# Ten dense projections per layer by seven half-size products each, with the sums of their weights added up in HBM by accumulating DMAs from GpSimd

## The reference

```python
for l in range(DEPTH):                      # DEPTH = 2
    h = rms_norm_2(x, norm_w[l])            # (256, 1024)
    x = x + hybrid_mixer(h, w_in[l], ...)

def hybrid_mixer(h, w_in, ...):
    proj = h @ w_in                         # (256, 1024) @ (1024, 5648)
    qkv, z_a, a_lg, b_lg, cf_val, cf_glu, z_b, gate_lg = jnp.split(proj, pts, axis=-1)
    qkv = jax.nn.silu(depthwise_conv_centred(qkv, qkv_conv_w))        # 5 taps
    ...                                     # gated delta rule, forward and backward -> o
    y_a = (o * silu(z_a)) @ w_dn_out        # (256, 512) @ (512, 1024)
    u = cf_val * jax.nn.sigmoid(cf_glu)
    u = depthwise_conv_centred(u, cf_conv_w) + cf_conv_b              # 31 taps
    u = jax.nn.silu(layer_norm_2(u, cf_ln_w, cf_ln_b))
    y_b = (u * jax.nn.silu(z_b)) @ w_cf_out
    gate = jax.nn.sigmoid(gate_lg + gate_b).reshape(bsz, seq, N_BRANCH, D_MODEL)
    y = gate[:, :, 0] * y_a + gate[:, :, 1] * y_b
    return y @ w_out
```

## Time and profile before

| | |
|---|---|
| Runs shown | 1493.84 and 1493.32 us, median 1493.58 |
| Span of the profiled execution | 1491.9 us, from the first to the last instruction |
| PE busy | 1459.9 us, 98% of the span |
| DVE, ACT, POOL busy | 57%, 30%, 21% |
| DMA | 184.4 MB at 124 GB/s on the mean |

### The profile page before, as it was taken

How to read it: one execution, slowest core, us unless ns; L and a number is a source line. 1 busy time by engine, 2 the same in 40 slices (tenths; PEclk the granted TensorE clock), 3 DMA queues, 4 the chain that set the end, 5 groups by cost and what they waited for, 6 DMA issues and landing times.

```text
span 1491.9 us, 21689 instructions
## 1 busy us (share of the span) xinstructions
PE 1459.9 (98%) x8912; PEld 1187.2 (80%) x8912; DVE 852.3 (57%) x1685; ACT 450.8 (30%) x905; POOL 311.3 (21%) x310
## 2 busy tenths in 40 slices
PE   7999999999999999999999999899999999999998
PEld 2677777667788888755968998788888888888887
DVE  1376666664544357623757744546688344677835
ACT  1232355424112121222326430233333213333321
POOL 0223302210666442131110402110100131010012
PEclk9999999999999999999999999999999999999999
DMA  9632232201322213331333353433332334333231
GB/s 387 255 139 113 114 113 114 114 29 54 143 95 98 92 57 116 144 113 57 114 113 114 114 227 113 159 143 139 114 115 100 123 130 154 128 114 115 113 114 43
DMA packets 17958, 184.39 MB, mean 124 GB/s; under 512 B 2370, under 2 KB 2882, under 8 KB 5316
## 3 DMA queue, kind: packets, MB, share of 16 engines
q1 hardware_dynamic: 17860, 183.01, 32.2%
HBM read 181.95 MB, written 1.05 MB: 123 GB/s over the span
## 4 chain that ended last, share of the span: by engine, by line
PE 89%; ACT 3%; DVE 3%; issue 1%; POOL 1%; DMA 1%; SPq 0%; DVEq 0%; POOLq 0%; ACTq 0%
PE ps L910 86%; PE ps L965 4%; DVE arena L2041 1%; DVE arena L2035 1%; DMA arena<-in_rp 1%; POOL arena L2848 1%; ACT arena L1559 0%; POOL arena L2852 0%; ACT L1995 0%; ACT L1993 0%; DMA arena<-in_wf 0%; DVE arena L2257 0%; DVE arena L2456 0%; ACT arena L1589 0%; ACT arena L1993 0%
## 5 line engine op out<-in xcount | busy, mean ns | idle before, releaser
L910 PE MATMUL ps<-arena 128*128 128x256 f32 (+7 forms) x8420 | 1411.5, 350 | 16.3 <-DMA arena<-in_wf 6.6
L910 PEld LDWEIGHTS ps<-arena 128*128 128x128 f32 (+4 forms) x8420 | 1133.9, 179 | 263.0 <-issue 126.6
L2848 POOL TENSOR_TENSOR arena<-arena 128x256 f32<-128x256 f32 (+6 forms) x254 | 280.3, 1124 | 855.3 <-DVE arena L2041 303.8
L2035 DVE TENSOR_TENSOR arena<-arena 128x512 f32<-128x512 f32 (+9 forms) x346 | 300.3, 893 | 176.1 <-ACT arena L1559 96.9
L1559 ACT ACTIVATE arena<-ps 128x512 f32<-128x512 f32 (+2 forms) x355 | 166.2, 489 | 569.9 <-PE ps L910 513.9
L2041 DVE SCALAR_TENSOR_TENSOR arena<-arena 128x256 f32<-128x256 f32 (+4 forms) x496 | 238.7, 532 | 106.7 <-ACT arena L1589 24.2
L2035 DVE TENSOR_TENSOR arena<-ps,arena 128x512 f32<-128x512 f32 (+16 forms) x157 | 64.5, 432 | 91.4 <-PE ps L910 81.4
L2041 DVE SCALAR_TENSOR_TENSOR arena<-arena,ps 128x256 f32<-128x256 f32 (+2 forms) x103 | 43.8, 439 | 80.7 <-PE ps L910 60.1
L965 PEld LDWEIGHTS ps<-arena 128*128 128x128 f32 x488 | 56.1, 142 | 33.5 <-issue 15.3
L965 PE MATMUL ps<-arena 128*128 128x128 f32 x488 | 73.4, 280 | 8.3 <-ACT arena L1559 5.5
L2038 DVE TENSOR_SCALAR arena<-arena 128x256 f32<-128x256 f32 (+10 forms) x179 | 62.1, 380 | 13.7 <-POOL arena L2848 10.8
(11 more groups left out here) (96 smaller groups left out, 299.8 us busy)
## 6 DMA issues: line engine op xcount, KB each, us to landing
arena<-in_wf SPq DMA_DIRECT2D x68, 2048.0 KB, 7.6
arena<-in_wf SPq DMA_DIRECT2D x22, 1024.0 KB, 6.5
arena<-in_first SPq DMA_DIRECT2D x3, 1024.0 KB, 20.6
arena<-in_wf SPq DMA_DIRECT2D x2, 1152.0 KB, 11.9
arena<-in_xin SPq DMA_DIRECT2D x4, 512.0 KB, 5.2
arena<-in_rp SPq DMA_DIRECT2D x2, 1024.0 KB, 10.1
arena<-in_consts SPq DMA_DIRECT2D x1, 1410.0 KB, 23.1
arena<-in_pa SPq DMA_DIRECT2D x2, 532.0 KB
```

The lines of the kernel that those rows point to most:

```text
L910: return e.matmul(o, l, r, start=start, stop=stop, skip_group_check=True)
L2035: return e.tensor_tensor(o, x, y, op)
L2848: return e.tensor_tensor(o, x, y, op)
```

## The change

Ten pieces of each b layer (`q1`, `q2`, `cv`, `cg`, `za`, `zb`, `m00`, `m10`, `m01`, `m11`, in this new order; `ab` and `q0` stay) are computed by seven products each. A product is 8 matmuls of 128 by 128 weights with 128 tokens, so a piece is 56 such matmuls in place of 32 with 256 tokens. A dense step is now two products (the fourth one only), and the order string stays. Products 6 and 5, 3 go on adding to the PSUM bank of product 1, and product 4 to that of product 7, after ACT has copied the value so far; DVE adds what belongs together (three adds of 128 x 256 a piece), and makes four sums of tokens (128 x 512 each) at the start of each layer.

The four sums of weights that the scheme wants for each piece (S1 to S4, 0.5 MB each) are made in HBM: GpSimd issues for two pieces at a time one plain DMA (HBM to HBM, 4 MB, one quarter of the weights written to all four sums) and three accumulating ones (3 MB, 3 MB and 1 MB), each after a wait for the one before. These 40 DMAs stand at fixed places of GpSimd's order: 13 and 12 in the two a layers (`KEEP_A`), one behind each of the groups of adds in their merges (`KEEP_M`), and 7 in the first b layer (`KEEP_B`). SP loads quarters and sums one by one, 70 loads of 0.5 MB in a b layer in place of 10 of 2 MB; the loads of sums of a pair of pieces wait for that pair's four DMAs. The ring is cut finer (14 places of 1024 columns), and from the first b layer on 12 places are left, the other two hold the sums of tokens. Beside this the squares of the second branch's layer norm go to four buffers in place of one, and some semaphores are shared.

```diff
-UNIT = 2048
-NU = 7
+UNIT = 1024
+NU = 14
...
+SEVEN_B = [("q1", "A"), ("q2", "A"), ("cv", "A"), ("cg", "C"), ("za", "T"), ("zb", "T"), ("m00", "G"), ("m10", "G"),
+           ("m01", "G"), ("m11", "G")]
+PARTS = {1: "11", 2: "12", 6: "S2", 7: "S3", 5: "S1", 4: "22", 3: "S4"}
+KEPT = {"S1": 0, "S2": 1024, "S4": 2048, "S3": 3072}
+RAW = {"22": 0, "11": 1024, "21": 2048, "12": 3072}
+KEEP = [f"b{l}{n}" for l in range(2) for n, _ in SEVEN_B]
+KEEP_AT_ONCE = 2
+
+KEEP_A = [{30: 1, 43: 1, 56: 1, 69: 1, 82: 1, 95: 1, 108: 1, 121: 1, 134: 1, 147: 1, 160: 1, 173: 1, 186: 1}, {10: 1, 25: 1, 40: 1, 55: 1, 70: 1, 85: 1, 100: 1, 115: 1, 130: 1, 145: 1, 160: 1, 175: 1}]
+KEEP_M = [1, 1]
+KEEP_B = [[2, 1, 3, 1], [0, 0, 0, 0]]
+
...
+def woven_b():
+
+    return sorted((7 * k + i, n, x[0], "W" + kind)
+                  for k, (n, kind) in enumerate(SEVEN_B) for i, x in enumerate(WINOGRAD))
...
+def dense_b():
+
+    steps = [[("ab", 0, "P")]] + [[("q0", c, "P")] for c in range(4)]
+    for k in range(0, 7 * len(SEVEN_B), 7):
+        steps += [[x[1:] for x in woven_b()[k + i:k + min(i + 2, 7)]] for i in range(0, 7, 2)]
+    return steps
+
...
+        TB = {n: r3(arena[:, 12 * UNIT + 512 * i:12 * UNIT + 512 * i + 512], 4) for i, n in enumerate("1234")}
...
+        kept = nc.dram_tensor("kept", (len(KEEP) * 128, 4096), F, kind="Internal").ap()
+        keeps = [range(n, min(n + KEEP_AT_ONCE, len(KEEP))) for n in range(0, len(KEEP), KEEP_AT_ONCE)]
+        d_keep = sem("d_keep")
...
+        short = [("a0gqk", "a0ma0", 8), ("a1ag", "a1mg1", 8), ("b0ab", None, 12)]
+        units = NU
+        rest_free = [None] * 3
         for name, w in PLAN:
             k = -(-w // UNIT)
...
+            for n, (begin, _, u) in enumerate(short):
+                if name == begin:
+                    rest_free[n] = [done_with[x] for x in tenant[u:] if x]
+                    tenant[u:], units = [f"rest{n}"] * (NU - u), u
             at = at if at + k <= units else 0
             count[at] += 16
-            pieces[name] = (ring[:, at * UNIT:at * UNIT + w], wf[off:off + 128 * w].rearrange("(p n) -> p n", p=128),
-                            (d_unit[at], count[at]), [done_with[x] for x in tenant[at:at + k] if x])
+            src, frees = places.get(name), [done_with[x] for x in tenant[at:at + k] if x]
+            if ":" in name:
+                whole, part = name.split(":")
+                n, at_raw = KEEP.index(whole), RAW.get(part)
+                if at_raw is not None:
+                    src = raw[128 * n:128 * n + 128, at_raw:at_raw + 1024]
+                else:
+                    src = kept[128 * n:128 * n + 128, KEPT[part]:KEPT[part] + 1024]
+                    frees.append(kept_by(n))
+            pieces[name] = (ring[:, at * UNIT:at * UNIT + w], src, (d_unit[at], count[at]), frees)
...
+            def one_of_seven_b(l, n, x):
+
+                w = use(f"b{l}{n}:{PARTS[x]}", 4)
+                t = [y[2] for y in WINOGRAD if y[0] == x][0]
+                if x in (1, 2, 7):
+                    b = bank("db", l, n, x)
+                else:
+                    b = psum("db", l, n, 7 if x == 4 else 1)
+                    p.wait_ge(db_copied(l, n, {6: 1, 5: 6, 4: 7, 3: 5}[x]))
+                if len(t) == 1:
+                    p.wait_ge(db_summed(l, "hs", "1324".index(t)))
+                    H = TB[t]
+                else:
+                    H = hB[:, 4 * int(t[0]) - 4:4 * int(t[0]), 128 * int(t[1]) - 128:128 * int(t[1])]
+                for c in range(2):
+                    for k in range(4):
+                        ins = mm(b[:, 128 * c:128 * c + 128], w[:, k, 128 * c:128 * c + 128], H[:, k, :],
+                                 x in (1, 2, 7) and c == k == 0, k == 3)
+                return ins
...
-                    if c:
-                        a.wait_ge(cf_pe.at(l, c))
-                    e.activation(UQ, CA[:, c, :], ACT.Square).then_inc(cf_act.hit(l, CF_SQ + c), 1)
+                    e.activation(CU[:, c, 0:256], CA[:, c, :], ACT.Square).then_inc(cf_act.hit(l, CF_SQ + c), 1)
...
+            def seven_copies_b(l, n, x, kind, last_th):
+
+                def event(y):
+                    return db_act.hit(l, BY_ACT_B[(n, y)])
+
+                def tanh(f, t, src, last_th):
+
+                    q = f"{f}{t}"
+                    if kind != "WG":
+                        a.wait_ge(last_th)
+                    if q != "12":
+                        a.wait_ge(db_summed(l, n, {"11": 2, "22": 5, "21": 4}[q]))
+                    done = event("t" + q if q != "12" else 3)
+                    if kind != "WG":
+                        e.activation(r3(THB[:, 256:512], 2), src, ACT.Tanh, scale=0.5).then_inc(done, 1)
+                        return db_summed(l, n, "g" + q)
+                    o = result_b(n, f, t)
+                    for c in range(2):
+                        g = 8 * int(n[1]) + 4 * int(n[2]) + 2 * f - 2 + c
+                        ins = e.activation(o[:, c, :], src[:, c, :], ACT.Tanh, scale=0.5, bias=gh[:, g:g + 1])
+                    ins.then_inc(done, 1)
+
+                if x in (2, 4):
+                    if x == 4 and kind != "WA":
+                        last_th = tanh(2, 2, result_b(n, 2, 2), last_th)
+                    return last_th
+                a.wait_ge(db_done(l, n, x))
+                b = r3(psum("db", l, n, 7 if x == 7 else 1)[:, 0:256], 2)
+                if x == 1:
+                    if kind == "WG":
+                        a.wait_ge(hb_pool.at(l, 2))
+                        if n != "m00":
+                            a.wait_ge(de_qd.at(l, 0), de_kq.at(l, 1))
+                        if n == "m11":
+                            a.wait_ge(cf_dve.at(l, CF_Y))
+                    copy(result_b(n, 1, 1), b).then_inc(event(1), 1)
+                elif x == 6:
+                    copy(result_b(n, 2, 1), b).then_inc(event(6), 1)
+                elif x == 7:
+                    k = [y for y, _ in SEVEN_B].index(n)
+                    a.wait_ge(db_summed(l, SEVEN_B[k - 1][0], 5) if k else db_summed(0, SEVEN_B[-1][0], 5) if l else None)
+                    copy(r3(EB, 2), b).then_inc(event(7), 1)
+                    if kind != "WA":
+                        last_th = tanh(1, 1, result_b(n, 1, 1), last_th)
+                elif x == 5:
+                    copy(result_b(n, 2, 2), b).then_inc(event(5), 1)
+                elif kind == "WA":
+                    copy(result_b(n, 1, 2), b).then_inc(event(3), 1)
+                else:
+                    last_th = tanh(2, 1, result_b(n, 2, 1), last_th)
+                    last_th = tanh(1, 2, b, last_th)
+                return last_th
+
...
+            def seven_sums_b(l, n, x, kind):
+
+                def event(y):
+                    return db_dve.hit(l, BY_DVE_B[(n, y)])
+
+                if x == 1 and n == SEVEN_B[0][0]:
+                    h11, h21, h12, h22 = (hB[:, 4 * k:4 * k + 4, 128 * t:128 * t + 128] for t in range(2) for k in range(2))
+                    v.wait_ge(hb_act.at(l, 3), hb_act.at(l, 4), hb_dve.at(l, 1), hb_dve.at(l, 2))
+                    v.wait_ge(*([db_done(0, SEVEN_B[-1][0], 3)] if l else rest_free[2]))
+                    for i, (y, a1, a2) in enumerate((("1", h11, h12), ("3", h12, h22), ("2", TB["1"], h22), ("4", h21, TB["2"]))):
+                        v.wait_ge(db_summed(l, "hs", i - 2 + i // 3) if i > 1 else None)
+                        done = db_dve.hit(l, BY_DVE_B[("hs", i)])
+                        if y == "2":
+                            stt(TB[y], a1, -1.0, a2, ALU.mult, ALU.subtract).then_inc(done, 1)
                         else:
...
+                            tt(TB[y], a1, a2, ALU.add if y == "4" else ALU.subtract).then_inc(done, 1)
...
+                def gated(f, t, src):
+                    q = f"{f}{t}"
+                    o = result_b("cv" if kind == "WC" else n, f, t)
+                    v.wait_ge(db_copied(l, n, "t" + q if q != "12" else 3))
+                    if kind == "WC":
+                        src = None
+                        v.wait_ge(db_copied(l, "cv", 3), db_summed(l, "cv", 4))
+                    stt(o, r3(THB[:, 256:512], 2), 1.0, src or o, ALU.add, ALU.mult).then_inc(event("g" + q), 1)
+
+                if x == 4 and kind in ("WT", "WC"):
+                    gated(2, 2, None)
+                if x in (2, 5, 4):
+                    f, t = {2: (1, 1), 5: (2, 2), 4: (2, 1)}[x]
+                    o = result_b(n, f, t)
+                    v.wait_ge(db_done(l, n, x), db_copied(l, n, {2: 1, 5: 5, 4: 6}[x]))
+                    tt(o, r3(EB if x == 5 else psum("db", l, n, 7 if x == 4 else 2)[:, 0:256], 2), o,
+                       ALU.add if x == 2 else ALU.subtract).then_inc(event(x), 1)
+                elif x == 7 and kind in ("WT", "WC"):
+                    gated(1, 1, None)
+                elif x == 3 and kind in ("WT", "WC"):
+                    gated(2, 1, None)
```

(23 more changed lines are left out.)

237 lines of the change are left out of this document (123 added, 114 removed).

## The result

The changed kernel takes **1616.84 us** (median of 2 runs, 1611.18 to 1622.5) where the kernel before takes 1493.58: **1.0814 times as long** (95% interval 1.0779 to 1.085). I forecast 1488, from 1460 to 1540; rival 1, on the slow side, gave 1550 and had a chance of 0.20. The profiled execution has a span of 1620.7 us, 128.8 over the one before. The runs of the kernel before that stand beside the experiments have medians of 1493.9 to 1496.6 us, up to 3 us above the 1493.6 of the table ahead, so a difference of two spans and a ratio of run times do not agree to better than that.

A forecast was written before the change was run, and what follows sets the result against it. PE's pace was taken to bound the kernel, with DVE nearly as full in places. Span 1491.9 - 32.7 + 8 + 2 + 4 - 3 + 10 + 2 + 4 = 1486.2 us, so 1488 us measured, range 1460 to 1540.

The forecast's parts named there:

- rival 1: GpSimd's DMAs hold the a layers up from about 25 us per 3 MB DMA on: 1550 us, chance 0.20.
- The DMAs of GpSimd: Waits behind them: +10 us at the second a layer's merge, +2 in linear attention, +4 at the `in_rp` load.
- the idle estimate: An accumulating 3 MB DMA of GpSimd takes 18 us, or 25 where weight loads hold the engines.
- The rule of two reads: An accumulating 3 MB DMA reads twice: 15 + 3 us, where a plain copy takes 10.
- PE's share, -32.7: Dense pieces of the b layers: 12.2 instead of 13.8 us each, 1.63 less for 20 pieces, -32.7 us.
- ACT "is hidden behind PE": b layers: ACT's 1 to 8 more instructions a piece cost nothing, with 1.7 us of another product as cover.
- The start of each b layer, +8: PE stands 4.1 us a layer before the sums of squares of q, k, v: +8 us for both layers.
- DVE full, +4: Between 1085 and 1145 us DVE's added adds overfill it: 2 us a layer given back, +4.
- tokens, +2: The four sums of tokens at each b layer's start cost 1 us a layer, +2 (0 to 7).
- Loads, 0: Weight loads in the dense run cost nothing: twelve places give 20 us of lead against some 7.6 us to land.
- rival 3: Weights come late in the b layers, 10 us a layer: 1500 to 1510 us, chance 0.13.
- Squares, -3: Second branch's norm: four buffers cut each round from 1.2 to 0.7 us, -3 us over both layers.

The follow-up runs named there:

- e1: Changed kernel without GpSimd's DMAs, raw quarters of weights loaded in place of the sums: 1551.39 us, 1.0372 times the kernel before.
- e2: Changed kernel with the accumulating DMAs of GpSimd made plain copies to the same places, same order and waits: 1.0521 times the kernel before.
- e3: Changed kernel with GpSimd's accumulating DMAs as plain copies, each to its own memory, so none waits for another of its pair: 1.0512 times the kernel before.
- e16: Kernel before the change with half of the matmuls of m00, m10 and m01 left out: 0.9924 times the kernel before, span 1483.0 us.
- e7: Kernel before the change, PE waiting in the middle of each whole dense piece of the b layers for the previous piece's copy: 1.0099 times the kernel before.
- e5: Changed kernel with each pair's tanh on ACT, and DVE's last two instructions on a pair, issued one pair later: 1.0731 times the kernel before.
- e8: e1 with DVE's three adds of a piece cut from 256 to 8 columns: 1.0346 times the kernel before, span 1546.9 us.
- e14: Kernel before the change with 12 instead of 14 ring places in the b layers: 1.0053 times the kernel before, span 1502.9 us.
- e15: Kernel before the change with only the squares of the second branch's norm put in four buffers: 1489.49 us, 0.9959 times the kernel before.
- e10: e1 with the tanh of each pair one pair later and m11 whole as before the change: 1.0203 times the kernel before, span 1523.8 us.
- e9: e1 with eight unused matmuls at each of six places where ACT's tanh waits, and one PE wait ahead: 1.0398 times the kernel before.

## Why the prediction was wrong

- **The DMAs of GpSimd** (my terms +10, +2, +4: 16 us; measured 66 less 3 for what e1 keeps). The mechanism, the place and the threshold of 25 us were right, and that is rival 1. Two steps failed. I took 18 us as likeliest, the idle estimate, although my own second figure for DMAs beside loads was 25; it is 25.5 (19.9 for the one without a load beside it), and from 18 to 25 us is what makes 47 us. That my +10 lay between the two, where 18 us make nothing late by my own working, hid the choice. And of the 15 to 16 us that the traffic costs (e2, e3 less e1) I had only the `in_rp` load, +4, which came as 4 to 7; that the weight loads of the a layers come later had no term.
- **The rule of two reads.** From the count of reads I had 15 + 3 us against 10 for a plain copy. The trace shows 25.5 against 18.2 us for 3 MB and 10.0 against 6.8 for 1 MB, 1.4 to 1.5 times, not twice; both are far from the copy at full rate. The Trainium skill's rule that a reducing transfer moves half of what a copy moves (Collectives: The Full Stack, "The bandwidth ceiling: the fold count and why AG ≠ RS ≠ AR"), which that page draws from rings of several ranks, had the right sign here and is too strong by these numbers. The difference of the two kinds is what separates e2 from the changed kernel, 47 us.
- **PE's share, -32.7.** The rate was nearly right: 32 records in 3.57 us, 0.112 each, so a piece is 12.5 us and 20 pieces would save 27, just below my range. The step that failed is the sentence ahead of it: "So the pace of PE sets the end, and a matmul less is time less". I took runs of matmuls without a break as proof that PE is the limit. Where DVE is 83 to 89% busy, such a run only says that both fit; e16 gives back 9 to 11 of 41 us.
- **ACT "is hidden behind PE"**: "each has 1.7 us of another product as cover". I named the cover and did not compare it with the 3.46 us of before, nor with what can stand ahead of a copy on ACT: a tanh that waits for some 4 us of DVE. Half the cover alone costs 14 to 15 us (e7), the place of the tanh 8 us a layer by the traces (e5).
- **The start of each b layer, +8; DVE full, +4; tokens, +2.** I had PE standing once, for the sums of squares. It stands there for 1.55 us, and before that three times for copies (7.5 us in the stretch), with the clock down behind it. The four sums of tokens hold PE up nowhere in this stretch of the second layer: its only wait for DVE, 0.7 us, was there before. DVE's added adds, on which most of these terms were built, are worth 3.8 us in all (e8).
- **Loads, 0; rival 3.** "Twelve places are 20 us of lead" held in the dense run, where PE waits for no load. It failed at the layer's end: in e14 the two places cost 11 us by the spans, 3 in the first and 8 in the second layer. I had looked at the rate, not at whose place the output weights get.
- **Squares, -3.** Right in sign, 5 us in size by the spans (e15).

Of the 56 us by which e1's b layers exceed before, e7 shows 15 and e14 11, e10 took 27 off in one step. These overlap, so they do not add up to it, and what the low clock costs by itself (mean 0.979 in e1, 0.998 before) is not separated: e9 shows only where it comes from. Why B stays 12 us over before in e10 is open in part: PE stands 12.6 us in it and not at all before, 7.0 of them for ACT's copies and 5.6 for DVE, but that its busy time there is no shorter than before (109 of 122 us, 110 of 110 before) is not explained.

## What to carry to other kernels

A long run of matmuls proves that PE is busy, not that it is the limit: before you book a saving there, ask how much the next engine has free in the same stretch, or take half of PE's work out and look. When a change splits a product, compare the time that covers a late release before and after with the longest thing that can stand ahead of that release in its engine's queue. A buffer taken out of a ring was paid for here where pieces of different size meet, at the end of a stage, not in the steady run.

## What the runs showed of the hardware

- A DMA that accumulates from HBM to HBM took 1.4 to 1.5 times as long as a plain one of its size in the same order of waits (25.5 to 18.2 us for 3 MB, 10.0 to 6.8 for 1 MB, e2). Without a load of SP beside it, 3 MB took 19.9 us accumulating and 13.9 to 15.7 plain. In e3, where several plain ones are under way at once, they took 19.4 (3 MB) and 9.8 us (1 MB).
- The record of an accumulating issue on POOL is 0.9 us (1 MB) to 1.7 us (3 MB) long, and 1.0 us for a plain one of 3 MB; the next add starts 0.6 and 1.1 us after the start of the accumulating ones.
- A plain copy of 4 MB took a median of 18.6 to 20.1 us, and 15.8 to 17.2 us in the changed kernel where no load ran beside it. Loads of 2 MB took 9.7 to 10.2 us beside plain DMAs and 11.0 beside the accumulating ones, instead of 7.6 to 8.0.
- Matmuls whose results nobody uses, in the place of a stop, kept the granted clock at 1.00 in that stretch and cost 1.8 of their 21 us.
